# One more row of a mixing product placed between the units of an attention loop (Trainium2, one core)

## What is computed

```python
proj = einsum('bsd,de->bse', rms_norm(h, g_pre_mix), w_in)
sq, sk, sv, rx, rg, cq, ck, cv = split(proj)
o_a = stick_breaking_attention(sq, sk, sv)      # 4 heads x 64, strictly causal
o_b = rg_lru(conv(rx), ...) * gelu(rg)          # recurrent block, width 512
o_c = sliding_window_sink_attention(cq, ck, cv) # 4 query heads
mixed = concatenate([rms_norm(o_a, ga), rms_norm(o_b, gb), rms_norm(o_c, gc)])
y = einsum('bse,ed->bsd', mixed, w_out)         # the mixing product
h = h + rms_norm(y, g_post_mix)
...                                             # MLP

# stick-breaking attention, query t, key s < t:
#   A[t,s] = sigmoid(z_ts) * prod_{s<j<t} sigmoid(-z_tj)
```

## Time and profile before

| | us |
|---|---|
| median of 3 runs | 1044.09 |
| lowest and highest of the 3 | 1043.96, 1046.66 |
| the profiled execution: its own time | 1043.6 |
| the profiled execution: its span | 1041.8 |
| PE busy | 1017.0 (98%) |
| DVE busy | 794.2 (76%) |
| ACT busy | 572.0 (55%) |
| mean granted TensorE clock | 0.996 of full |

### The profile page before, as it was taken

One profiled execution on the slowest core, in us unless ns is written; L12 is line 12 of the kernel. 1 busy time (PEld: TensorE's weight loads), 2 busy tenths in 40 slices (PEclk: granted clock), 3 DMA queues, 4 the chain that ended last, 5 costly groups with the idle time before them and its releaser, 6 DMA issues.

```text
span 1041.8 us, 12454 instructions
## 1 busy us (share of the span) xinstructions
PE 1017.0 (98%) x4982; PEld 820.8 (79%) x4982; DVE 794.2 (76%) x737; ACT 572.0 (55%) x751; POOL 88.4 (8%) x70
## 2 busy tenths in 40 slices
PE   9999999998989999999999999999999999999996
PEld 7878777886757787788788888788888788888784
DVE  6237659698578578877878867998776998777998
ACT  7423432658758536777663557333657333666454
POOL 0013213021312142000000000000000000000000
PEclk9999999999999999999999999999999999999998
DMA  9411111200011544013013022022031031035004
GB/s 341 142 60 41 41 41 41 81 1 1 7 36 42 174 180 173 1 43 119 1 51 111 1 82 81 1 83 78 1 121 41 1 121 41 1 123 201 1 0 162
DMA packets 38657, 74.65 MB, mean 72 GB/s; under 512 B 3236, under 2 KB 12744, under 8 KB 38600
## 3 DMA queue, kind: packets, MB, share of 16 engines
q1 hardware_dynamic: 38456, 73.83, 20.4%
q10 hardware_dynamic: 144, 0.03, 0.0%
HBM read 65.46 MB, written 8.39 MB: 71 GB/s over the span
## 4 chain that ended last, share of the span: by engine, by line
PE 87%; DVE 5%; ACT 3%; DMA 2%; issue 1%; SPq 1%; ACTq 0%; DVEq 0%
PE ps L719 27%; PE ps L723 26%; PE ps L721 26%; PE ps L934 2%; PE ps L888 2%; DMA y<-in_x 2%; PE ps L792 1%; PE ps L959 1%; DVE out_gained L2101 1%; DVE y L2159 1%; DMA xt<-in_x_turned 1%; DVE y L2050 1%; ACT sb_w L1332 1%; PE ps L1036 1%; PE ps L823 1%
## 5 line engine op out<-in xcount | busy, mean ns | idle before, releaser
L719 PE MATMUL ps<-b_op,a_op 128*128 128x512 f32 x448 | 174.6, 390 | 3.6 <-issue 3.6
L719 PE MATMUL ps<-a_op,b_op 128*128 128x512 f32 x448 | 175.4, 392 | 2.5 <-issue 1.4
L723 PE MATMUL ps<-a_op,b_op 128*128 128x512 f32 x448 | 174.4, 389 | 0.0
L721 PE MATMUL ps<-a_op,b_op 128*128 128x512 f32 x448 | 174.3, 389 | 0.0
L723 PE MATMUL ps<-b_op,a_op 128*128 128x512 f32 x448 | 174.3, 389 | 0.0
L721 PE MATMUL ps<-b_op,a_op 128*128 128x512 f32 x448 | 174.3, 389 | 0.0
L1486 ACT CAST a_op<-f 128x1024 fp32r<-128x1024 f32 x56 | 58.8, 1049 | 112.9 <-PE ps L723 72.7
L2007 DVE TENSOR_TENSOR b_op<-wq,b_op 128x1024 fp32r<-128x1024 f32 x96 | 116.9, 1217 | 0.0
L719 PE MATMUL ps<-act_hi,w_hi 128*128 128x512 f32 x288 | 114.6, 398 | 0.8 <-DVE act_lo L1682 0.8
L723 PE MATMUL ps<-act_hi,w_lo 128*128 128x512 f32 x288 | 112.2, 389 | 0.0
L721 PE MATMUL ps<-act_lo,w_hi 128*128 128x512 f32 x288 | 112.1, 389 | 0.0
(11 more groups left out here) (225 smaller groups left out, 1680.7 us busy)
## 6 DMA issues: line engine op xcount, KB each, us to landing
wq<-in_w_ff_in SPq DMA_DIRECT2D x16, 1024.0 KB, 5.4
wq<-in_w_ff_out SPq DMA_DIRECT2D x16, 1024.0 KB, 5.1
stage<-in_w_in SPq DMA_DIRECT2D x16, 512.0 KB, 4.6
y<-in_x SPq DMA_DIRECT2D x4, 1024.0 KB, 13.2
stage<-in_w_out SPq DMA_DIRECT2D x8, 512.0 KB, 3.8
h_spill<-y SPq DMA_DIRECT2D x8, 512.0 KB, 2.7
h_back<-h_spill SPq DMA_DIRECT2D x2, 2048.0 KB, 11.9
out<-y SPq DMA_DIRECT2D x8, 512.0 KB, 2.8
```

The source lines that it names most:

```text
L719: nc.tensor.matmul(dst, stat[0], mov[0], start=first, stop=False, skip_group_check=chained)
L721: nc.tensor.matmul(dst, stat[0], mov[1], start=False, stop=False, skip_group_check=chained)
L723: return nc.tensor.matmul(dst, stat[1], mov[0], start=False, stop=last, skip_group_check=chained)
```

## The change

One more row is put into the loop, in unit 7, so `N_EARLY` goes from 14 to 15 and only row 15 is left behind the loop. Every unit from 8 on holds the row one number higher than before. In units 7, 8 and 9 the first half of the row is issued ahead of `weighted(u-1)` instead of behind it; in units 7 and 8 the second half follows at once instead of standing behind `head_turn(2u+1)`. The load of the activation table moves from n = 29 of ACT's loop to behind the loop, ahead of `output_copy(3)`. With `N_EARLY`, the PSUM banks of rows 15 and later and the counts that DVE's sums are waited for at move by one.

```diff
         WINDOW_ROWS = 2
-        FILL_UNITS = (0, 1, 2, 3, 4, 5, 8, 9, 10, 11, 12, 13)
+        FILL_UNITS = (0, 1, 2, 3, 4, 5, 7, 8, 9, 10, 11, 12, 13)
         N_EARLY = WINDOW_ROWS + len(FILL_UNITS)
         SUM_UNIT, SPLIT_HEADS = 6, (7, 21)
+
+        ROW_AHEAD, WHOLE_ROW = (7, 8, 9), (7, 8)
...
             for u in range(len(UNITS)):
                 head_turn(2 * u)
+                if u in ROW_AHEAD:
+                    recurrent_out(row_of(u), range(2))
+                if u in WHOLE_ROW:
+                    recurrent_out(row_of(u), range(2, OUT_K))
                 if u:
                     weighted(u - 1)
-                if u in FILL_UNITS:
+                if u in FILL_UNITS and u not in ROW_AHEAD:
                     recurrent_out(row_of(u), range(2))
                 if u + 2 < len(UNITS):
                     scores(u + 2)
                 head_turn(2 * u + 1)
-                if u in FILL_UNITS:
+                if u in FILL_UNITS and u not in WHOLE_ROW:
                     recurrent_out(row_of(u), range(2, OUT_K))
...
                 if n == SPLIT_HEADS[1]:
                     split_hi(N_IN + 2, N_IN % 2)
-                if n + LEAD == HEADS:
-                    nc.scalar.preload_act_table_set("natural_log_exp_and_others")
+            nc.scalar.preload_act_table_set("natural_log_exp_and_others")
             output_copy(len(UNITS) // CHAIN - 1)
```

## The result

| | before | after |
|---|---|---|
| median, us (5 runs each, side by side) | 1043.96 | 1049.1 |
| lowest and highest | 1043.33, 1046.66 | 1048.69, 1050.07 |
| the profiled execution, its own time | 1043.6 | 1048.69 |

What follows compares the result with a forecast made beforehand. PE, busy 98% of the span, bounds the kernel. A 2.75 us shift of the ACT and POOL chain less 0.75 us slack gives +2.0 us: 1045.6 us profiled, median 1046.1 us, range 1043.4 to 1048.3.

Steps and rivals of the forecast that it cites:

- Unit 7: Row 8 ahead of weighted(6): the added row costs PE 0.15 us, bounds 0 and 2.5 us; scores(9) at full clock.
- Rival E: Unit 7: the clock falls in spite of row 8; up to 2.35 us on top, 1048.4 us; chance 0.06.
- Units 8 and 9: Waits for ACT's copies ahead of head_turn(18) and row 10 make PE 2.45 us later at head_turn(20), one more row done.
- The loop's end: Sums wait for POOL at 361.45 instead of 359.41; nothing is left of the 2.8 us PE no longer has to do.
- C: Change of pairs: unit 9's waits don't bite, PE at most 0.3 us late; 1043.7 us; chance 0.20.
- D: Loop's end is PE's own: 2.8 + 0.5 us gained, less 0.15; 1040.9 us; chance 0.03.
- F: Behind the loop the table load holds ACT about its own length more: 1.3 us on top, 1047.4 us; chance 0.04.
- B: Clock falls to 1.2 GHz behind the loop, or in unit 9's hole at the same 1.5 us: 1047.6 us; chance 0.22.
- The hole and the slow clock pay for it: Unit 7: the idle time and slow scores ahead of scores(9) cover the added row, leaving PE 0.15 us later.

Runs made afterwards that it cites:

- ahead7_tail: The changed kernel with only unit 7's row whole and ahead; behind the loop two window parts, two stick parts, then the sums: 1.0007 of before, 1045.24 us.
- ahead7: The changed kernel with only unit 7's row whole and ahead; units 8 and 9 as in the kernel before: 1.0031 of before, 1047.33 us.
- after_again: The changed kernel measured once more, unaltered, in another session: 1.0038 of before, 1047.92 us.
- ahead78: The changed kernel with row 10 put back behind weighted(8) in unit 9; units 7 and 8 keep rows ahead: 1.0029 of before, 1047.07 us.
- fill_7: The kernel before with five matmuls of unused result in unit 7's hole ahead of scores(9): 0.9998 of before, 1043.96 us.
- new_dve: Against before: unit 6's sums in unit 5, row 8 whole in unit 6, late table load, four parts ahead of tail sums, DVE's addition before split: 0.9985, 1043.55 us.
- ahead7_dve: ahead7_tail with DVE's first addition of row 16 placed ahead of the low halves' split: 0.9981 of before, 1042.92 us.

## Why the prediction was right or wrong

**Unit 7: size right, where the clock holds.** Scores(9) were forecast for 304.1 to 305.85 and started at 303.96 at full clock. ahead7_tail has M0 to M1 of 21.56 without a slow stretch: +0.2 on the 21.35 of before, forecast 0.15. (One reading was loose: PE doesn't idle from the sums to 302.42; weighted(6) stands between, and the hole is the 1.28 us of the earlier trace rows.) But the clock held in only five of the ten profiles with this row ahead in unit 7. Rival E, at 0.06, was priced at up to 2.35 us, where ahead7 against ahead7_tail shows 1.59.

**Units 8 and 9: right.** M0 to M1 of after_again is 2.65 longer than before, forecast 2.45. Row 9 whole costs 24.44 - 1.59 - 21.56 = 1.29 (forecast 1.16 for head_turn(18), from 314.94 to 316.1, with unit 7's 0.15 in it), row 10's wait 24.00 - (24.44 - 1.59) = 1.15 (forecast 1.3). The 1.59 is unit 7's slow stretch, from ahead7 against ahead7_tail, which have the same loop.

**The loop's end: right.** The forecast had PE 2.45 us late at head_turn(20) and the sums 2.0 us late, so that M1 to M2 would shrink by 0.45 us; it shrinks by 0.40. POOL's sum sets the end, and nothing of the 2.8 us is left. Rivals C and D are out: row 10 waited, and the sums came late. F is out as well: the output copy stands at 355.45, at the end of the load. The drain of about 1380 ns that the Trainium skill ("ScalarE: Activation LUTs", section "What ACT_TABLE_LOAD costs") gives beside the load isn't seen at this place: in after's trace the copy before it ends at 354.15, the load runs from 354.16 to 355.44, and the next copy starts at 355.45.

**The clock: wrong, and this is the step that failed.** The sum had nothing for a fall of the clock: it took "From 361.45 on the order is that of before", and gave the clock's fall behind the loop (B) 0.22 at 1.5 us. The mechanism was named rightly and priced rightly: M2 to M3 grew by 1.64 to 1.7 us. But it came in both profiles of after and in those of ahead7 and ahead78. Its argument against, a stretch at 342 to 351 with 1.0 us of idle time and full clock, was no match: no one-column matmuls stand there, and its longest hole is 0.83 us (before 350.73). The right neighbour was the hole ahead of scores(9): 1.84 us of one-column matmuls and 1.28 us of idle time there, 1.95 and 1.22 us here. The picture had been drawn in the forecast, then not believed. (In the order of things the two differ: in unit 7 the hole follows the sums, here it precedes them.)

**Two holes are not one case.** The slow stretch in unit 9, named under B as an alternative ("the same price holds"), came as well in the profile of after, and not in after_again: M0 to M1 of 25.34 against 24.00, 1.34 us. The range's high end held one fall, the truth up to two: 2.25 (waits, M0 to M2) + 1.64 + 1.34 = 5.2 against the 5.26 found between the marks. (The 1.34 is itself the difference of the two profiles, so this sum tests only the others.) No one-column matmuls stand near unit 9's stretch; it follows two holes of 1.16 and 1.06 us around seven transposes, and the same two holes didn't bring it on in after_again. Its cause stays open. Without it the same kernel took 1047.92 us, within the stated range; so that the time left the range is the second fall, which by their mean clock four of the five executions of after_again didn't have.

**The base.** The profiled execution of before itself held a slow stretch that cost 1.45 us (fill_7 against it). "The hole and the slow clock pay for it" thus spends money that only such executions have: against an undisturbed 19.90, unit 7's row costs 1.66 us (21.56), not 0.2.

## What to carry to other kernels

A hole on TensorE beside matmuls of one column can cost more than its own length, since the clock may fall behind them; when a change turns such a place from "just in time" into "waits 1 us", price the fall as the likely case, and each such hole by itself. A place without a hole isn't safe for that: the clock fell right behind the one-column sums of ahead7 with 0.18 us of idle time, and behind those of new_dve with none. When work leaves an engine's tail, look at what stands first in the queue behind it: here the gain of 2.8 us was held by the one-column sums that wait for another engine, and came through, 2.5 us of it where the clock held, only when independent products stood ahead of them and the instruction that frees a bank stood ahead of one that was blocked anyway. And before a slow stretch is counted as payment for an edit, ask whether all executions have it; the spread of times beside their mean clock tells.

## What the hardware showed that I had not expected

The same binary shows different slow stretches from one execution to the next (after: U9 and end, after_again: end alone), and the kernel before spreads over 1042.0 to 1047.2 us with its mean granted clock between 0.999 and 0.993. A stretch of 3 to 4 us at 1.2 GHz cost 1.3 to 1.6 us where PE was the bound, one of 10 us in units 7 and 8 cost 3.3 us. What decides whether unit 7 or unit 9 falls in a given execution stays open; so does the share of executions in which each falls, which the profiles taken here are too few to give. Not tried: the order of ahead7_dve with matmuls in the last 0.27 us hole.
